# Nine bursts of plain fp32 products instead of thirteen in two pairs of heads

## The chip, the cores and the metric

The kernel runs on one core of one Trainium2 chip. The metric is the device time of one execution in microseconds (us); lower is better. The core has a tensor engine (TensorE, PE in the profile), a vector engine (VectorE, DVE), a scalar engine (ScalarE, ACT), GpSimd (POOL) and SyncE (SP), which issues the transfers. Each engine runs its own queue of instructions in order and meets the others by semaphores.

## The reference

One layer of a streaming encoder over 4096 tokens of width 1024, all in float32:

```python
h = rms_norm(x, norm_g)
proj = einsum('bsd,de->bse', h, w_in)         # 5376 columns
(qa, ka, va, za, qb, kb, vb, zb, ga, gb) = split(proj, ...)
ya = swa_sink_attention(rope(qa), rope(ka), va, a_sinks) * silu(za)   # 8 q heads, 2 kv heads, own chunk + 1 back
yb = chunked_relpos_attention(qb, kb, vb, b_rel_bias) * silu(zb)      # 8 heads, own chunk + 8 back
merged = sigmoid(ga + gate_bias0) * (ya @ w_br_a) + sigmoid(gb + gate_bias1) * (yb @ w_br_b)
out = rms_norm(x + merged @ w_out, final_g)
```

A chunk is 64 tokens and a head 64 wide. Branch A sees a window of two chunks and has a sink term in its softmax; branch B sees nine chunks and adds a bias by relative position.

## The kernel before

The sequence is worked in eight blocks of 512 tokens (`NBLK`), each block four query tiles of 128 (`TT`). The first and last block are written out, the six between run in a loop (`blocks`, L639). The projections are made with two-part numbers: each factor is split into a high part and a rest in the type fp32r, and three products (hi hi, lo hi, hi lo; L909 to L911, L876 to L878 and L851 to L853) stand for one fp32 product. In what follows R is one such product of 512 columns. A weight tile is worked in four quarters of six R each; a quarter is the step `("mm", tile, quarter)`.

The attention is made in plain fp32. Heads are taken two at a time: four A pairs (sets 0 to 3) and four B pairs (sets 4 to 7), in the order 0, 4, 1, 5, 2, 6, 3, 7 (`ORDER`). For a pair TensorE makes
- S, `scores` (L944 for A, L953 for B): the score tile of one query tile, into the PSUM tiles `sc`; the VectorE shapes it (mask, bias) and takes the row maxima (L1242 to L1268), the ScalarE makes the exponentials (`exps`, L1146), which are E in the plan and free the score tile;
- T, `turn_p` (L973): up to four 128x128 transposes of the probabilities into `ps_pt`. ScalarE (L1153) or VectorE (L1329), as `A_OUT` and `B_OUT` say, copies them into a ring of four tiles `probs_t`. A turn waits until the turn before it is copied out;
- V, `values` (L1004): products of the turned probabilities with the values, summed in `ps_o`. A V step takes the key blocks of one entry of `A_BURSTS` or `B_BURSTS`. V3 of an A pair takes two. The first V of a pair waits until the pair before has been read out of `ps_o` (`whole`, L1366);
- N, `norm` (L1013): four transposes of the reciprocal sums into an accumulator bank, from which VectorE makes `gate` (L1360).

The order of all this is written out by hand. `block_plan` (L130) makes one list of steps, `PLAN`, and every engine walks the same list and issues its own part of each step. `A_BEATS` (L119) and `B_BEATS` (L120) are the beats of one pair: T, V, S and E as above with their numbers, F the next quarter of a weight tile from the list `fill`, G and H the gating of the pair before, D the denominators. S and E in a pair's beats belong to the next pair. `norm` is put in by a rule: after the fourth F or later, when the quarter left its tile open. Twelve F belong to a pair. Jobs that hang on a tile travel with its quarters: after the last quarter of a q tile of branch A ScalarE makes `pre` and `pre_hi` (L1098, L1101); the next tile's first quarter carries `rope_in` (VectorE: L1304, L1308) and its third the rope products (TensorE: L1024, L1025). A rope product takes the bank that `norm` used last, and waits till `gate` has read it. For the second A pair (set 1) these are the rope of q2, in tile z5.

`check_ring` (L345) holds the plan to the rule that a turn's ring slot has been read by its V step four turns later.

Of the kernel before, what the change touches and what calls it, by code (L numbers as in the profile page):

```python
# [24 lines left out]
D = 1024  # L25
# [90 lines left out]
O_BANKED = 2  # L116


A_BEATS = "T0 F G T1 V0 F H D T2 V1 S0 F E0 T3 V2 F S1 V3 F E1 F F S2 F E2 F F S3 F E3 F"  # L119
B_BEATS = "F T0 F G T1 F H D T2 V0 F T3 F T4 V1 S0 F T5 E0 F T6 V2 S1 F T7 E1 F T8 V3 S2 F T9 E2 V4 S3 T10 F E3 V5 F V6"  # L120
BEATS_QUARTERS = 12
NORM_AFTER = 4
EARLY = 1
# [6 lines left out]
def block_plan():  # L130
# [45 lines left out]
    for n, s in enumerate(ORDER):  # L176
        nxt = ORDER[n + 1] if n + 1 < SETS else None
        quarters = 0
        for beat in (A_BEATS if s < PAIRS else B_BEATS).split():
            kind, no = beat[0], int(beat[1:] or 0)  # L180
# [1299 lines left out]
```

## Time and profile before

| | before |
|---|---|
| median of three executions | 3417.24 us (3415.64 to 3418.3) |
| profiled execution, its own time | 3415.78 us |
| its span from first to last instruction | 3414.0 us |
| TensorE matmuls busy | 3342.3 us, 98% |
| VectorE, ScalarE, GpSimd busy | 1488.9, 1422.8, 1306.6 us |
| mean granted TensorE clock | 0.999 |

Busy TensorE time is made of modelled ends and contains overlaps of neighbouring matmuls; the time from one start to the next is what a matmul takes of the span. A row of the timeline has the start and the duration in us, the engine, the line of the kernel, the operation, output and inputs, the shapes, how many instructions of the same kind were merged into the row, and in brackets the idle time before it with what ended it.

### The profile page before, as it was taken

What the parts mean: (1) busy time and instruction counts of PE and PEld (TensorE: products, weight loads), DVE (VectorE), ACT (ScalarE), POOL (GpSimd) and SP (SyncE); (2) the same over time, 40 slices, a digit from 0 to 9 for tenths busy, and PEclk for the clock granted to TensorE, in tenths of its full rate; (3) what the DMA queues carried; (4) which work ended last, traced back from release to release, by engine and by line L of the source; (5) the groups of instructions that cost most, each with busy time, mean ns of one, the idle gap of its engine ahead of it and who ended that gap; (6) DMA issues with size and microseconds to landing.
All of it is one profiled execution on the core that took longest, in us unless ns stands there. A gap on an engine that the chain in (4) does not pass through costs nothing.

```text
span 3414.0 us, 48305 instructions
## 1 busy us (share of the span) xinstructions
PE 3342.3 (98%) x16328; PEld 2498.0 (73%) x16328; DVE 1488.9 (44%) x3097; ACT 1422.8 (42%) x2969; POOL 1306.6 (38%) x1087
## 2 busy tenths in 40 slices
PE   8999999999999999999999999999999999999998
PEld 6667876678766787667876678766787667876676
DVE  4662355513555135551355513555135551355512
ACT  4443444434444344443444434444344443444432
POOL 3334442345423454234542344423454234542244
PEclk9999999999999999999999999999999999999999
DMA  4222431224311242112421124311242112521123
GB/s 156 62 62 87 172 99 50 62 87 167 99 50 62 87 168 99 50 62 87 168 99 52 61 86 168 98 56 61 83 172 94 55 60 84 173 93 56 56 82 116
DMA packets 97782, 319.53 MB, mean 94 GB/s; under 512 B 9984, under 2 KB 26624, under 8 KB 95360
## 3 DMA queue, kind: packets, MB, share of 16 engines
q1 hardware_dynamic: 97536, 316.34, 28.4%
q8 instruction: 144, 2.36, 0.3%
q14 instruction: 102, 0.84, 0.1%
HBM read 299.52 MB, written 16.78 MB: 93 GB/s over the span
## 4 chain that ended last, share of the span: by engine, by line
PE 85%; issue 6%; DVE 5%; POOL 2%; ACT 1%; DMA 0%; DVEq 0%; POOLq 0%; SPq 0%; ACTq 0%
PE acc L909 16%; PE acc L911 14%; PE acc L910 14%; PE ps_o L1004 6%; PE ps_pt L973 5%; PE sc L953 4%; PE sc L909 3%; PE sc L910 3%; PE sc L911 3%; POOL w_lo L755 2%; PE sc L944 2%; PE sc L851 2%; PE sc L852 2%; PE sc L853 2%; PE sc L876 1%
## 5 line engine op out<-in xcount | busy, mean ns | idle before, releaser
L755 POOL TENSOR_TENSOR w_lo<-w_raw,w_hi 128x512 fp32r<-128x512 f32 x928 | 1209.2, 1309 | 2060.0 <-ACT w_hi L1058 2059.3
L909 PE MATMUL acc<-h_hi,w_hi 128*128 128x512 f32 x2432 | 1010.4, 415 | 2.4 <-DVE q L1316 2.4
L911 PE MATMUL acc<-h_hi,w_lo 128*128 128x512 f32 x2432 | 952.7, 392 | 0.0
L910 PE MATMUL acc<-h_lo,w_hi 128*128 128x512 f32 x2432 | 950.4, 391 | 0.0
L1058 ACT ACTIVATE w_hi<-w_raw 128x512 fp32r<-128x512 f32 x928 | 574.2, 624 | 392.9 <-DMA w_raw<-w 116.5
L909 PEld LDWEIGHTS acc<-h_hi,w_hi 128*128 128x128 f32 x2432 | 456.3, 188 | 212.3 <-issue 133.9
L911 PEld LDWEIGHTS acc<-h_hi,w_lo 128*128 128x128 f32 x2432 | 456.4, 188 | 101.5
L910 PEld LDWEIGHTS acc<-h_lo,w_hi 128*128 128x128 f32 x2432 | 458.1, 188 | 75.7
L1146 ACT ACTIVATE probs_b<-sc,negm 128x640 f32<-128x640 f32 x256 | 203.2, 794 | 373.6 <-DVE negm L1263 373.0
L1153 ACT ACTIVATE probs_t<-ps_pt 128x512 f32<-128x512 f32 (+1 forms) x272 | 150.7, 554 | 264.8 <-PE ps_pt L973 264.8
L1288 DVE SCALAR_TENSOR_TENSOR part<-th,sc 128x512 f32<-128x512 f32 x64 | 43.9, 686 | 468.0 <-PE sc L911 467.8
L1329 DVE COPY probs_t<-ps_pt 128x512 f32<-128x512 f32 (+1 forms) x188 | 125.3, 666 | 250.8 <-PE ps_pt L973 250.3
L1263 DVE TENSOR_REDUCE negm<-sc 128x1 f32<-128x640 f32 x256 | 211.0, 824 | 8.9
L909 PE MATMUL sc<-y_hi,w_hi 128*128 128x512 f32 x512 | 201.5, 394 | 6.0 <-DVE y_lo L1376 6.0
L911 PE MATMUL sc<-y_hi,w_lo 128*128 128x512 f32 x512 | 199.4, 389 | 0.0
L910 PE MATMUL sc<-y_lo,w_hi 128*128 128x512 f32 x512 | 199.3, 389 | 0.0
L973 PE MATMUL ps_pt<-ident,probs_b 128*128 128x128 f32 x1200 | 187.0, 274 | 6.2 <-DVE probs_t L1329 6.2
L973 PEld LDWEIGHTS ps_pt<-ident,probs_b 128*128 128x128 f32 x1200 | 147.6, 141 | 52.9 <-DVE probs_t L1329 8.6
L1255 DVE TENSOR_TENSOR sc<-sc,bias 128x256 f32<-128x256 f32 (+2 forms) x512 | 184.3, 360 | 3.0
L1116 ACT ACTIVATE th<-acc,gb_half 128x512 f32<-128x512 f32 x128 | 88.1, 688 | 218.4 <-PE acc L911 218.4
L1004 PE MATMUL ps_o<-probs_t,v_b 128*64 128x512 f32 (+1 forms) x960 | 175.9, 455 | 1.0 <-DVE probs_t L1329 0.3
L953 PE MATMUL sc<-k_b,q 64*128 64x320 f32 (+3 forms) x992 | 164.3, 448 | 3.6 <-ACT probs_b L1146 3.6
(140 smaller groups left out, 3923.8 us busy)
## 6 DMA issues: line engine op xcount, KB each, us to landing
w_raw<-w SPq DMA_DIRECT2D x464, 512.0 KB, 3.5
rows<-x SPq DMA_DIRECT2D x36, 512.0 KB, 7.4
xt<-x_t SPq DMA_DIRECT2D x16, 1024.0 KB, 10.0
out<-rows SPq DMA_DIRECT2D x32, 512.0 KB, 2.8
x_in<-x SPq DMA_DIRECT2D x28, 512.0 KB, 5.4
cs<-rope_tab SPq DMA_DIRECT2D x8, 512.0 KB, 4.3
bias<-near SPq DMA_DIRECT2D x1, 1024.0 KB, 13.3
g_out<-final_g SPq DMA_DIRECT2D x1, 512.0 KB, 11.5
```

Source lines behind the costliest of these rows:

```text
L755: pool.tensor_tensor(w_lo[n % 2][:, c], w_raw[n % 2][:, c], w_hi[n % 2][:, c].bitcast(FP32), ALU.subtract).then_inc(w_split, 1)
L909: pe.matmul(dst[:, :], hi, src_hi[:, k, :], start=begin, stop=False)
L910: pe.matmul(dst[:, :], hi, src_lo[:, k, :], start=False, stop=False)
L911: mm = pe.matmul(dst[:, :], lo, src_hi[:, k, :], start=False, stop=end)
L953: mm = pe.matmul(sc[hh][:, c, lo:B_HALF], q[n % 2][rows_, t * P:(t + 1) * P], k_b[rows_, s - PAIRS, t * P + c * B_HALF + lo:t * P + (c + 1 ...
L973: mm = pe.transpose(ps_pt[:, col + (t - t0) * P:col + (t - t0 + 1) * P], weights_of(s, hh, t)[:, r * P:(r + 1) * P], ident[:, :])
L1004: mm = pe.matmul(ps_o[HD * hh:HD * hh + HD, t0 * P:(t0 + n) * P], val, ring(first, turn)[:, col:col + n * P], start=j == every[0], stop=j ...
L1058: act.activation(w_hi[n % 2][:, c], w_raw[n % 2][:, c], ACT.Copy).then_inc(w_hi_done, 1)
L1146: act.activation(p_, score_tile(s, hh, t), ACT.Exp, bias=negm[:, POS[s] % 2, c:c + 1], accum_out=sums[:, POS[s] % 2, c:c + 1]).then_inc(pr ...
L1153: act.activation(ring(first, turn)[:, 0:n], ps_pt[:, 0:n], ACT.Copy).then_inc(pt_out[0], 1)
L1255: dve.tensor_tensor(dst, dst, tab, ALU.add).then_inc(scores_shaped, 1)
L1263: dve.tensor_reduce(nm, score_tile(s, hh, t), AX.XY, ALU.max, negate=True).then_inc(neg_ready, 1)
```

## The change

Two strings of beats are replaced. No function and no other constant is changed.

```diff
-A_BEATS = "T0 F G T1 V0 F H D T2 V1 S0 F E0 T3 V2 F S1 V3 F E1 F F S2 F E2 F F S3 F E3 F"
-B_BEATS = "F T0 F G T1 F H D T2 V0 F T3 F T4 V1 S0 F T5 E0 F T6 V2 S1 F T7 E1 F T8 V3 S2 F T9 E2 V4 S3 T10 F E3 V5 F V6"
+A_BEATS = "T0 F G T1 F H D T2 V0 V1 S0 F E0 T3 F F S1 V2 V3 F E1 F S2 F E2 F F S3 F E3 F"
+B_BEATS = "F T0 F G T1 F H D T2 F T3 F V0 V1 S0 T4 F T5 E0 F T6 V2 S1 F T7 E1 F T8 V3 S2 F T9 E2 V4 S3 T10 F E3 F V5 V6"
```

In an A pair V0 moves behind T2, directly ahead of V1; V2 moves behind S1, directly ahead of V3; and one F moves from between E1 and S2 to ahead of S1. In a B pair V0 moves from behind T2 to ahead of V1, T4 moves from ahead of V1 to behind S0, and V5 moves behind the last F, directly ahead of V6. Counted as stretches with V or S between two F, an A pair has four instead of six and a B pair five instead of seven.

## Rows read from the trace of the kernel before

**Rows 1.** Page of the profile: busy time by engine, and granted clock in 40 slices.
```profile
PE 3342.3 (98%) x16328; PEld 2498.0 (73%) x16328; DVE 1488.9 (44%) x3097; ACT 1422.8 (42%) x2969; POOL 1306.6 (38%) x1087
...
PEclk9999999999999999999999999999999999999999
```
**Rows 2.** TensorE's timeline (start, us, line, operands, count): four turns between products R.
```profile
562.54 0.39 PE L910 MATMUL acc<-h_lo,w_hi 128*128 128x512 f32 x1
562.77 0.40 PE L911 MATMUL acc<-h_hi,w_lo 128*128 128x512 f32 x1
563.00 0.60 PE L973 MATMUL ps_pt<-ident,probs_b 128*128 128x128 f32 x4
563.35 0.48 PE L909 MATMUL acc<-h_hi,w_hi 128*128 128x512 f32 x1
563.67 0.39 PE L910 MATMUL acc<-h_lo,w_hi 128*128 128x512 f32 x1
```
**Rows 3.** TensorE's timeline: a lone V step of one key block between products R.
```profile
588.69 0.40 PE L911 MATMUL acc<-h_hi,w_lo 128*128 128x512 f32 x1
589.02 0.65 PE L1004 MATMUL ps_o<-probs_t,v_b 128*64 128x256 f32 x4
589.60 0.50 PE L909 MATMUL acc<-h_hi,w_hi 128*128 128x512 f32 x1
589.94 0.40 PE L910 MATMUL acc<-h_lo,w_hi 128*128 128x512 f32 x1
```
**Rows 4.** TensorE's timeline: turns, then a V step, then S0 of the next pair.
```profile
536.83 0.60 PE L973 MATMUL ps_pt<-ident,probs_a 128*128 128x128 f32 x4
537.36 0.65 PE L1004 MATMUL ps_o<-probs_t,v_a 128*64 128x256 f32 x4
537.94 1.35 PE L953 MATMUL sc<-k_b,q 64*128 64x320 f32 x8
```
**Rows 5.** TensorE's timeline: a V step of two key blocks, then turns.
```profile
590.88 0.39 PE L911 MATMUL acc<-h_hi,w_lo 128*128 128x512 f32 x1
591.20 0.66 PE L1004 MATMUL ps_o<-probs_t,v_b 128*64 128x128 f32 x8
591.79 0.66 PE L973 MATMUL ps_pt<-ident,probs_a 128*128 128x128 f32 x4
...
592.52 0.39 PE L910 MATMUL acc<-h_lo,w_hi 128*128 128x512 f32 x1
```
**Rows 6.** TensorE's timeline: V0 of the third A pair; T4 of the third B pair.
```profile
595.02 0.65 PE L1004 MATMUL ps_o<-probs_t,v_a 128*64 128x256 f32 x4 [0.75 <-DVE whole L1366]
...
630.13 0.40 PE L911 MATMUL acc<-h_hi,w_lo 128*128 128x512 f32 x1
630.70 0.55 PE L973 MATMUL ps_pt<-ident,probs_b 128*128 128x128 f32 x3 [0.18 <-DVE probs_t L1329]
```
**Rows 7.** Timelines of TensorE, ScalarE and VectorE in the second A pair, S0 being in Rows 4.
```profile
543.41 1.35 PE L953 MATMUL sc<-k_b,q 64*128 64x320 f32 x8
549.91 0.49 PE L1024 MATMUL acc<-pre_hi,perm_r 128*128 128x512 f32 x1 [1.17 <-DVE gate L1360]
...
544.75 0.63 ACT L1101 ACTIVATE pre_hi<-pre 128x512 fp32r<-128x512 f32 x1
548.50 0.19 ACT L1146 ACTIVATION_READ_ACCUMULATOR probs_b<-sc,negm 128x1 f32 x1
...
544.86 0.11 DVE L1252 MEMSET sc<- 64x64 f32 x1 [2.55 <-PE sc L953]
547.70 0.68 DVE L1304 TENSOR_TENSOR pre_lo<-pre,pre_hi 128x512 fp32r<-128x512 f32 x1
549.09 0.68 DVE L1360 TENSOR_TENSOR gate<-acc,z 128x512 f32<-128x512 f32 x1
```
**Rows 8.** TensorE's timeline: S1 and S2 in the first A pair of a block.
```profile
484.41 1.35 PE L953 MATMUL sc<-k_b,q 64*128 64x320 f32 x8
491.04 1.35 PE L953 MATMUL sc<-k_b,q 64*128 64x320 f32 x8
```

## The prediction

> **What bounds the kernel.** The page comes first: TensorE is busy 98% of the span, VectorE 44%, ScalarE 42%, GpSimd 38%, and the granted clock is in its highest tenth in all forty slices, so the 2.4 GHz level [rows 1]. A step on another engine is therefore worth only the wait that it gives TensorE; a step on TensorE is worth its own time. The change moves no instruction out of the kernel, so the question is what TensorE loses between instructions. For that I read its timeline by starts, not by durations (the durations overlap: products start every 0.23 us and are shown as 0.39). Then I read ScalarE's and VectorE's timelines at the places where the order changes.
>
> **What a burst costs.** In a run of split products (R, 512 columns) starts are 0.23 us apart. A burst of four turns T between two R takes 562.77 to 563.67, 0.90 us from the R before to the second R after, of which 2 x 0.23 is what two R cost anyway: 0.44 for four turns, 0.11 each [rows 2]. A lone `values` step V takes 588.69 to 589.94, 1.25 us, less 0.46 for two R: 0.79. Its own columns are 4 x 256, at 2.4 GHz 0.43 us. So 0.36 us is spent in getting in and out: 0.10 before V (0.33 from R to V against 0.23), 0.16 behind its columns (0.59 to the next start against 0.43), 0.10 in the first R behind it (0.34 against 0.23) [rows 3]. Next to a turn V saves nothing: 0.53 from T to V is the turns' 0.44 and again 0.09, and V to the score tile S is 0.58 [rows 4]. But inside one V step there is no such gap: V6 of a B pair is two key blocks, eight pieces of 128 columns (V3 of an A pair has the same form), the same 0.43 us of columns, and the next group starts 0.59 us after it, as it does after a V of one block. A burst in which T follows the V takes 590.88 to 592.52, 1.64 us, less 0.46, 0.44 and 0.43: 0.31, so T behind V gives back 0.05 [rows 5].
>
> **The plan, part by part.** I wrote out both plans step by step. The instructions are the same; what changes is the neighbours.
> - A pairs: V0 goes from behind T1 to in front of V1, and V2 from behind T3 to in front of V3 (one F, a quarter tile of six R, moves ahead of S1). Two V steps lose their borders.
> - B pairs: V0 and V1 become neighbours behind F, with T4 now behind them; V5 moves next to V6. In the last B pair of a block V5 and V6 are neighbours already.
> - So a block has 4 x 2 + 3 x 2 + 1 = 15 joins V-V. Block 0 leaves out V steps without keys: 8 + 3 = 11. In all 7 x 15 + 11 = 116 joins.
>
> The trace has no V-V border with a wait between the steps. Its cost lies between 0 (the border inside V6, whose loads and products are of the same shape) and 0.16 (V to another kind) [rows 5]. I take 0, the nearest row, so each join saves 0.36 [rows 3]: 116 x 0.36 = 41.8 us. T4 stands behind products in 4 B pairs of 7 blocks: 28 x 0.05 = 1.4 us.
>
> A page rule speaks against this. The Trainium skill, TensorE: Matmul & The Clock Gate, section Part 3 (Packing small matmuls), says that a weight load overlaps running matmuls only when its row group differs; neighbouring V steps use all rows, so by it their loads would not hide. By that page the border V-V would stay unhidden and the rival with 0.16 per join would be right; the eight pieces of [rows 5], whose stationary operands change within the step with no time lost, speak against it.
>
> **Waits that go.** V0 of the third A pair waits for VectorE's `whole` with 0.75 us idle, one of eight such rows [rows 6]. In the new plan V0 stands a quarter tile and four turns later (1.8 us), so 8 x 0.75 = 6.0 us go. T2, which is next, needs T1's copy: VectorE makes it directly behind `whole`, and V5's 0.43 us ahead of T0 put T1 later relative to the chain that starts at the q tile's end, so nothing is late there. In the third B pair T4 starts 0.57 us after the last R instead of 0.23, because T3's copy on VectorE is late; seven such rows [rows 6]. Now V0 (0.8 us and more) lies between: 7 x 0.34 = 2.4 us go. T4 to T5 is now turns, one F and `norm`, no less than T0 to T1, where the same ScalarE copy is in time.
>
> **A wait that grows.** A step list per engine shows one change of order on VectorE: in the second A pair the F that carries `rope_in` for q2 moves ahead of S1, so its two VectorE operations (L1304, L1308) are now queued ahead of the shaping of S1. Behind them wait S1's maxima, its exponentials, `norm`'s product (`gate`, L1360), and for that the rope product on TensorE (L1024), which needs its bank. S0 to S1 is 5.47 us and S0 to the rope product 11.97 [rows 4, 7]. ScalarE finishes `pre_hi` at 544.75 + 0.63 = 545.38 (it is behind S0's exponentials, which do not move). L1304 then starts at 545.42; the two operations hold VectorE 1.39 us (547.70 to 549.09), so the shaping starts at 546.81 instead of 544.86, takes its 2.84 us (544.86 to 547.70), `gate` starts at 549.65 and the rope product 0.82 us behind that, at 550.47. That is 12.53 us after S0, 0.56 later than before, where the sum above booked a gain of 0.36 for the join V2-V3. Correction 0.92 x 8 blocks = 7.4 us. TensorE itself would be there 10.3 us after S0 (5.47 - 0.79 + 1.37 to S1, then the 5.69 of the next part less one F), so it is this chain that counts.
>
> ScalarE has one change: a split of the next weight tile stands ahead of tile 1's exponentials in each A pair. It fits into the idle time before these (they wait for VectorE), so it costs nothing; uncovered it would cost some 0.6 us, as long as `pre_hi` of the same shape takes [rows 7]. GpSimd's and SyncE's orders are unchanged.
>
> **The distance that gets short.** In A pairs S2 waits for the exponentials of tile 1, and S1 to S2 shrinks: 6.63 us now, less six R (1.37), plus V2 (0.43): 5.69 [rows 8]. S1 to the end of those exponentials is 543.41 to 548.69, 5.28 us [rows 7]. 0.41 us are left, so I book nothing. In the second pair the rope wait hides it. This is the thinnest cover, 32 times in the kernel.
>
> **Sum.** 41.8 + 1.4 + 6.0 + 2.4 - 7.4 = 44.2 us. The profiled execution's span is 3414.0 us and its own time 3415.8, 1.5 below the median of 3417.2. From the span 3369.8, from the median 3373.0 us.
>
> **Rivals.**
> 1. V-V keeps a border of 0.16 us. For it: every border of V to something else has it, and the second V has a wait in front. Against: the border inside V6. 116 x 0.16 = 18.6 us less gain: 3391.6 us.
> 2. S2 comes late in A pairs. If the chain from S1 grows by 0.75 us (one more 0.7 us operation on VectorE), 32 x (0.75 - 0.41) = 11 us: 3384 us. For it: 0.41 us is less than one VectorE operation. Against: the per-engine order shows none added but in the second pair.
> 3. The rope chain costs nothing, because `rope_in` turns out earlier than I read: 3365.6 us. Against: ScalarE is behind S0's exponentials.
> 4. The change does not do what it says: the 0.36 us belongs to each V step, wherever it stands. Then only the waits move, 6.0 + 2.4 - 7.4: 3416 us. Against: the 0.10 in front and the 0.10 behind lie outside the V.
> 5. Slower: the chain S1, maxima, exponentials, S2 becomes the bound of every A pair. It decides from 44.2 / 32 + 0.41 = 1.8 us of added chain; with the two operations of the second pair (1.39) and one more product like L1360 (0.68) ahead of S1 everywhere it would be 2.07: 32 x 1.66 = 53 us lost against 44.2 gained, 3426 us. Against: only one pair of four carries a `rope_in` there.
>
> **Chances.** Forecast 0.67; rival 1 0.14; rival 2 0.09; rival 3 0.05; rival 4 0.03; rival 5 0.02. The range reaches from rival 3 to rival 1 with some 2 us of error on either side: 3363 to 3394 us. A measurement of this kernel can tell about 0.2% (7 us) from no change; faster by more than that is the forecast and rivals 1 to 3, 0.95; within it rival 4, 0.03; slower rival 5, 0.02.
>
> **What would show it.** In the profile after, V1 of an A pair should start 0.43 us behind V0; 0.59 there is rival 1. The third A pair's 0.75 wait and T4's wait should be gone. The wait of the rope product for `gate` should grow from 1.17 to some 2.3 us. S2 of A pairs should show no wait for `probs_b`; one of 0.3 is rival 2. The clock should stay in its highest tenth. I would be wrong if a copy out of `ps_pt` or the ring of four came late at a place where I read only the order.

## The result and the profile after

| | before | after |
|---|---|---|
| median of five executions | 3416.75 us | 3398.23 us (3396.62 to 3398.9) |
| ratio to before | | 0.9945, 95% interval 0.9932 to 0.9958 |
| span of the profiled execution | 3414.0 us | 3396.7 us |
| mean granted TensorE clock | 0.999 | 0.994 |

The change makes the kernel 18.5 us faster. The forecast was 44.2 us faster, and the time lies outside its range of 3363 to 3394 us. The page after, first the busy time by engine, then the granted clock in 40 slices:

```profile
PE 3314.0 (98%) x16328; PEld 2511.9 (74%) x16328; DVE 1491.5 (44%) x3097; ACT 1423.9 (42%) x2969; POOL 1310.7 (39%) x1087
...
PEclk9999999999999999999999999999999999999999
```

Against [rows 1] nothing stands out. 85 us slices do not show what lasts 3 us, and TensorE is still called 98% busy. The mean clock of 0.994 beside 0.999 is the first hint: half a percent of the span is 17 us, which is some 34 us more at half the clock.

**The joins came as forecast.** TensorE's timeline after, second A pair (T2 V0 V1 S0, then S1 V2 V3), and second to last the join V0 V1 of the first B pair:

```profile
536.80 0.60 PE L973 MATMUL ps_pt<-ident,probs_a 128*128 128x128 f32 x4
537.33 1.08 PE L1004 MATMUL ps_o<-probs_t,v_a 128*64 128x256 f32 x8
...
544.42 1.35 PE L953 MATMUL sc<-k_b,q 64*128 64x320 f32 x8
545.70 1.09 PE L1004 MATMUL ps_o<-probs_t,v_a 128*64 128x256 f32 x12
546.72 0.50 PE L909 MATMUL acc<-h_hi,w_hi 128*128 128x512 f32 x1
...
512.41 1.94 PE L1004 MATMUL ps_o<-probs_t,v_b 128*64 128x512 f32 x8
514.28 0.59 PE L944 MATMUL sc<-k_a,q 64*128 64x192 f32 x4
```

V2 and V3 are one row of twelve instructions and take 545.70 to 546.72, 1.02 us. Their columns are 2 x 0.43, and what is left is the one exit of 0.16 known from [rows 3]. The B join takes 1.87 us to the next start for 8 x 512 columns (1.71) and again 0.16. So the border V-V costs nothing, with a satisfied wait between the steps.

**The rope product of the second A pair lost it.** VectorE's, GpSimd's and TensorE's timelines after, the place of [rows 7]:

```profile
545.82 0.72 DVE L1304 TENSOR_TENSOR pre_lo<-pre,pre_hi 128x512 fp32r<-128x512 f32 x1 [3.10 <-ACT pre_hi L1101]
546.64 1.59 DVE L1308 TENSOR_TENSOR pre<-pre,cs 128x512 f32<-128x512 f32 x1
548.31 0.11 DVE L1252 MEMSET sc<- 64x64 f32 x1
551.14 0.68 DVE L1360 TENSOR_TENSOR gate<-acc,z 128x512 f32<-128x512 f32 x1
...
546.38 1.30 POOL L755 TENSOR_TENSOR w_lo<-w_raw,w_hi 128x512 fp32r<-128x512 f32 x1 [0.40 <-ACT w_hi L1058]
...
551.95 0.66 PE L1024 MATMUL acc<-pre_hi,perm_r 128*128 128x512 f32 x1 [3.14 <-DVE gate L1360]
```

S0 starts at 538.35 here, so the rope product stands 13.60 us behind it; the forecast said 12.53, and before it was 11.97. L1304 starts 7.47 us after S0, where 7.48 was forecast. L1308 takes 1.59 us instead of the 0.69 that goes with its shape: GpSimd's w_lo began at 546.38 and ends at 547.68, and L1308 ends 0.55 us later. From there everything is one chain: shaping, `gate`, rope product. TensorE is idle for 3.14 us, not the 2.3 forecast and not the 1.17 of before.

**And then the clock fell.** The same place one block later, after:

```profile
975.35 0.79 PE L1024 MATMUL acc<-pre_hi,perm_r 128*128 128x512 f32 x1 [3.14 <-DVE gate L1360]
976.36 0.63 PE L909 MATMUL acc<-h_hi,w_hi 128*128 128x512 f32 x1
976.79 0.63 PE L910 MATMUL acc<-h_lo,w_hi 128*128 128x512 f32 x1
...
978.95 1.35 PE L953 MATMUL sc<-k_b,q 64*128 64x320 f32 x8
```

Two R start 0.43 us apart where 0.23 is usual. The rope product to S2 takes 3.60 us; with the clock up it is 2.01 (before: 549.91 to 551.92). The views of chosen windows, the 3 us from the rope product on, for two blocks of the kernel after and then one of the kernel before. The third number from the right is the granted clock:

```profile
975.40:978.40 3.00, 3.00 (x7) 2.44 (x8) 1.38 (x2) 0.66 (x3) 1.28 (x1) 0.50 0.02 5
2246.60:2249.60 3.00, 3.00 (x16) 2.09 (x16) 1.83 (x2) 0.69 (x3) 1.29 (x1) 1.00 0.02 5
```

```profile
549.90:552.90 3.00, 2.99 (x16) 2.11 (x16) 1.66 (x2) 0.00 (x0) 1.92 (x2) 1.00 0.41 106
```

A clock of 0.50 is 1.2 GHz. It fell behind this wait in six of the eight blocks after and in none before; in two blocks the same idle time of 3.1 us left it up. What a fall costs is read from the rope product to that of the third pair, TensorE's timeline after, first a block with a fall and then one without:

```profile
1822.54 0.79 PE L1024 MATMUL acc<-pre_hi,perm_r 128*128 128x512 f32 x1 [3.14 <-DVE gate L1360]
1873.12 0.50 PE L1024 MATMUL acc<-pre_hi,perm_r 128*128 128x512 f32 x1
...
2246.58 0.49 PE L1024 MATMUL acc<-pre_hi,perm_r 128*128 128x512 f32 x1 [3.15 <-DVE gate L1360]
2294.32 0.50 PE L1024 MATMUL acc<-pre_hi,perm_r 128*128 128x512 f32 x1
```

That is 50.58 us against 47.74. Two blocks (1822.54 and 2669.08) lose 2.85 us in this way, and their clock stands at half for some 6.7 us; the other four falls last some 3.4 us and cost 1.5 to 1.6 us each. The six together are 11.9 us.

### The profile page after: what moved, and what is told of

It is laid out like the page before. It is cut to its first block, busy times and chain, and to the rows that moved or that the text cites. A ratio compares the mean times of both kernels' runs of the same rounds, so it can differ in the third digit from the quotient of the medians.

```text
span 3396.7 us, 48305 instructions
## 1 busy us (share of the span) xinstructions
PE 3314.0 (98%) x16328; PEld 2511.9 (74%) x16328; DVE 1491.5 (44%) x3097; ACT 1423.9 (42%) x2969; POOL 1310.7 (39%) x1087
## 4 chain that ended last, share of the span: by engine, by line
PE 82%; issue 9%; POOL 4%; DVE 3%; ACT 2%; DMA 0%; POOLq 0%; DVEq 0%; SPq 0%; ACTq 0%
PE acc L909 15%; PE acc L911 14%; PE acc L910 14%; PE ps_o L1004 5%; PE ps_pt L973 5%; POOL w_lo L755 4%; PE sc L953 4%; PE sc L909 3%; PE sc L911 3%; PE sc L910 3%; PE sc L944 2%; PE sc L853 1%; PE sc L852 1%; PE sc L851 1%; PE sc L876 1%
## 5 line engine op out<-in xcount | busy, mean ns | idle before, releaser
L1146 ACT ACTIVATE probs_a<-sc,negm 128x256 f32<-128x256 f32 x256 | 120.1, 474 | 109.5 <-DVE negm L1268 108.8
```

The lines of the kernel that those rows point to most:

```text
L1146: act.activation(p_, score_tile(s, hh, t), ACT.Exp, bias=negm[:, POS[s] % 2, c:c + 1], accum_out=sums[:, POS[s] % 2, c:c + 1]).then_inc(pr ...
```

## The experiments

The theory was: the joins and the vanished waits are worth what was forecast (51.6 us), and the loss is in one place per block, in two parts, the longer wait of the rope product and the clock behind it. The rival: the joins are worth about half, everywhere, which would give 18 us just as well.

**One string at a time.** `B_BEATS` alone:

```diff
+B_BEATS = "F T0 F G T1 F H D T2 F T3 F V0 V1 S0 T4 F T5 E0 F T6 V2 S1 F T7 E1 F T8 V3 S2 F T9 E2 V4 S3 T10 F E3 F V5 V6"
```

> Only B_BEATS is changed, A_BEATS is that of before. Theory (each join V-V saves 0.36 us; the loss sits at the rope product of the second A pair, which this kernel leaves alone): 52 joins x 0.36 + 28 x 0.05 + seven T4 waits x 0.34 = 22.5 us faster than before, 3392 to 3397 us, so faster than the changed kernel although it makes half of the change; the rope product's wait stays at 1.17 us and the granted clock at 0.999. Rival (each join saves only half as much, everywhere): some 12 us faster than before, 3402 to 3407 us.

Measured: 3391.41 us, 24.8 us faster than before (ratio 0.9927, 0.9909 to 0.9944), and 7 us faster than the whole change; that is 0.6 us below the band of 3392 to 3397. The rope product waits as before and the clock is 0.999:

```profile
547.82 0.49 PE L1024 MATMUL acc<-pre_hi,perm_r 128*128 128x512 f32 x1 [1.17 <-DVE gate L1360]
```

`A_BEATS` alone:

```diff
+A_BEATS = "T0 F G T1 F H D T2 V0 V1 S0 F E0 T3 F F S1 V2 V3 F E1 F S2 F E2 F F S3 F E3 F"
```

> Only A_BEATS is changed, B_BEATS is that of before. Theory (64 joins x 0.36 + 8 V0 waits x 0.75 = 29 us gained, 8 x 3.6 = 29 us lost at the rope product of the second A pair: 1.6 by its wait, 1.6 by the clock behind it, 0.36 of a join's gain that is covered): no change to 4 us slower, 3413 to 3421 us; wait of the rope product about 3.1 us, clock about 0.52 in the 2 us behind it. Rival (each join saves half): 9 us faster, 3405 to 3410 us.

Measured: 3423.01 us, 6.8 us slower than before (ratio 1.0019, 1.0009 to 1.0029), 2 us beyond the band. The clock fell behind the rope product in all eight blocks, not six:

```profile
553.98 0.79 PE L1024 MATMUL acc<-pre_hi,perm_r 128*128 128x512 f32 x1 [3.15 <-DVE gate L1360]
```

Half of the change holds more than the whole gain, the other half is a loss; together they give 24.8 - 6.8 = 18.0 us, the 18.5 of the whole. The rival falls by the B half: half-priced joins would have given it some 12 us, and no rope wait hides anything there.

**GpSimd taken out of the way.** The changed kernel with ScalarE's order of before:

```diff
-... S1 V2 V3 F E1 F S2 ...
+... S1 V2 V3 E1 F F S2 ...
```

> The changed kernel with E1 ahead of the F in A_BEATS (S1 V2 V3 E1 F F S2): nothing moves on TensorE or VectorE; on ScalarE the split of the next weight tile goes back behind tile 1's exponentials, and so GpSimd's w_lo goes away from VectorE's rope operations. Theory (L1308 took 1.59 us instead of 0.69 because it ran into a w_lo on GpSimd): L1308 0.7 us, rope product 12.5 us after S0 instead of 13.6, wait 2.1 us. If the clock then holds its upper level 8 x 2.6 = 21 us faster than the changed kernel, 3375 to 3380 us; if it still falls 8 x 1.0: 3388 to 3392 us. Rival (L1308 is slow for another reason): 3398 us and a wait of 3.1 us.

Measured: 3384.98 us, 13 us less than the change. VectorE's, GpSimd's and TensorE's timelines:

```profile
545.88 0.69 DVE L1308 TENSOR_TENSOR pre<-pre,cs 128x512 f32<-128x512 f32 x1
...
543.96 1.27 POOL L755 TENSOR_TENSOR w_lo<-w_raw,w_hi 128x512 fp32r<-128x512 f32 x1 [6.90 <-ACT w_hi L1058]
551.09 1.30 POOL L755 TENSOR_TENSOR w_lo<-w_raw,w_hi 128x512 fp32r<-128x512 f32 x1 [5.86 <-ACT w_hi L1058]
...
550.30 0.49 PE L1024 MATMUL acc<-pre_hi,perm_r 128*128 128x512 f32 x1 [2.24 <-DVE gate L1360]
```

No w_lo lies beside L1308 and it takes 0.69 us again; the wait is 0.9 us shorter. So the 0.9 us were the collision, set off by the one split that the forecast priced at nothing. The time lies between the two bands given, because the clock neither held everywhere nor fell everywhere: behind the rope product it fell in four of eight blocks (the first, whose wait is 3.77 us, and three of the seven with 2.2 us). Two of these windows:

```profile
550.30:553.30 3.00, 3.00 (x16) 2.10 (x16) 1.84 (x2) 1.23 (x4) 2.21 (x2) 1.00 0.02 5
971.10:974.10 3.00, 2.97 (x10) 1.96 (x11) 1.82 (x2) 1.26 (x4) 2.18 (x2) 0.69 0.02 5
```

**VectorE's order of before.** The changed kernel with `rope_in` of set 2 one quarter later:

```diff
-            fill[at_] = [*fill[at_], ("rope_in", s)]
+            late = at_ + (s == 2)
+            fill[late] = [*fill[late], ("rope_in", s)]
```

> The changed kernel with rope_in of the second A pair one quarter later, so behind S1's shaping in VectorE's order, as in the kernel before; ScalarE's order stays changed. Theory: shaping starts 1.45 us after S1, rope product 6.5 us after S1 (as before: 543.41 to 549.91), so about 12.55 us after S0 instead of 13.6, wait 2.1 to 2.2 us, clock held: 3375 to 3381 us. Rival (the order on VectorE alone costs nothing, only its collision with GpSimd, which may come back at another operation): 3385 us or more.

Measured: 3381.42 us (ratio 0.99, 0.9883 to 0.9918), half a microsecond above the band. The rope product:

```profile
547.17 0.50 PE L1025 MATMUL acc<-pre_hi,perm_r 128*128 128x512 f32 x1 [2.10 <-DVE gate L1361]
```

The wait is 2.10 us, as expected of this run, and the clock fell in three of eight blocks. So with either repair the step that the forecast had worked out (12.53 us after S0, 2.3 us of wait) is there (12.56 us here, 12.71 with GpSimd out of the way); but even that wait is long enough for the clock to fall now and then, a cost that it did not have.

**The wait itself taken away.** The changed kernel with that `rope_in` behind S1 and the rope product one weight tile later, where `norm`'s product has long been read:

```diff
-            fill[at_] = [*fill[at_], ("rope_in", s)]
+            late = at_ + (s == 2)
+            fill[late] = [*fill[late], ("rope_in", s)]
+            at_ += 4 * (s == 2)
             fill[at_ + 2] = [("rope", s), *fill[at_ + 2]]
```

> The changed kernel with rope_in of the second A pair behind S1 (as in rope_in_late) and the rope product one weight tile later, behind S3, where norm's product has long been read; the first A pair has the same pattern. Theory (the loss is all in the wait of the rope product and the clock that falls behind it): no wait of 2 us at the rope product, clock 0.999, in its place 0.3 to 0.5 us at the next tile's claim as in the first pair; 8 x 2.2 - 8 x 0.4 + the clock of three of eight blocks (3 x 1.6) = 19 us below rope_in_late, 3358 to 3367 us. Rival (another wait takes its place, at S2 or S3 of that pair): 3372 us or more.

Measured: 3360.74 us, inside the band of 3358 to 3367, 55.8 us faster than before (ratio 0.9836, 0.9822 to 0.9849) and 37 us faster than the change. The rope product follows its score tile with no wait, and a short one stands at the next tile's claim:

```profile
549.77 1.35 PE L955 MATMUL sc<-k_b,q 64*128 64x320 f32 x8
551.05 0.50 PE L1026 MATMUL acc<-pre_hi,perm_r 128*128 128x512 f32 x1
...
554.86 0.49 PE L911 MATMUL acc<-h_hi,w_hi 128*128 128x512 f32 x1 [0.35 <-DVE q L1318]
```

The same move of the rope product in the kernel before, to price it apart:

```diff
+            at_ += 4 * (s == 2)
             fill[at_ + 2] = [("rope", s), *fill[at_ + 2]]
```

> The kernel before with its rope product of the second A pair one weight tile later, nothing else. It takes the wait of 1.17 us (1.4 us against an unhindered start) and may bring 0.3 to 0.5 us at the next claim: 8 x 1.0 = 8 us faster than before, 3406 to 3412 us. It prices what the change and the move of the rope product do apart from each other: if theory holds, the joins and the two other waits (51.6 us) stand on top of it.

Measured: 3409.24 us, inside the band and 7.4 us faster than before (ratio 0.9978, 0.9969 to 0.9988). The two kernels without the rope wait differ by 3409.24 - 3360.74 = 48.5 us, and the forecast's sum without its rope term is 41.8 + 1.4 + 6.0 + 2.4 = 51.6. That is the change's own worth outside the rope product, and it is right within 3 us.

**Which resource the wait hung on.** The rope product moved, but `rope_in` left ahead of S1 and the split ahead of E1:

```diff
+            at_ += 4 * (s == 2)
             fill[at_ + 2] = [("rope", s), *fill[at_ + 2]]
```

> The changed kernel with the rope product one weight tile later, but rope_in still ahead of S1 on VectorE and the split still ahead of E1 on ScalarE. The bank no longer waits, but S1's shaping is still late by 1.4 us for the two operations and 0.9 us for GpSimd. Theory: the chain S1, maxima, exponentials, S2 is then 7.5 us against 5.7 us of TensorE's work, so S2 of that pair waits some 1.8 to 2.0 us for probs_b (the forecast's rival 2 in one pair of four) and the clock falls behind it in about two to four of eight blocks: 3376 to 3386 us. Rival (only the bank mattered): no wait at S2, same as rope_later, 3358 to 3367 us.

Measured: 3388.69 us, some 3 us above the band. The bank no longer matters and S2 waits in its place:

```profile
551.17 1.35 PE L954 MATMUL sc<-k_b,q 64*128 64x320 f32 x8 [2.00 <-ACT probs_b L1147]
```

Behind these 2.0 us the clock fell in four of seven blocks, and in the first, where the wait is 3.59 us. The late shaping of S1 is one cause with two receivers: take the bank away and the exponentials are next. It is the forecast's rival 2, in the one pair of four that the per-engine order had pointed to.

## Why the prediction was wrong, step by step

- *A lone V has 0.36 us around it and a join saves all of it*: right. The border V-V is 0, as the pieces within one V had shown; rival 1 and the page's rule that loads hide only where row groups differ (the Trainium skill, TensorE: Matmul & The Clock Gate, Part 3) do not hold for these steps. The B half gave 24.8 us where 18.7 + 1.4 + 2.4 = 22.5 stood; the 2.3 us more are not traced.
- *The waits of V0 and T4 go*: right, no row of either is left after.
- *S2 keeps 0.41 us in A pairs*: right in the running blocks. In the first block, where VectorE has more to fill in, S2 of the first pair waits 0.95 us against 0.24 to 0.28 in the kernels with the A pairs of before.
- *The rope product 12.53 us after S0*: its place and mechanism were right, its size was not. It measured 13.60, 1.07 us more in each block, 8.6 us in all.
- *ScalarE's split ahead of E1 costs nothing*: **this step failed**. I asked whether ScalarE had idle time for it, and it had. I did not follow what the split sets off: GpSimd's w_lo, 1.30 us, now beside a VectorE operation on the critical chain. With the split back in its place L1308 takes 0.69 us instead of 1.59 and the wait 2.24 us instead of 3.14: 0.9 of the 1.07 us in each block. The kernel before shows the same collision, in the rows under this list. I read durations of each engine in its own lane and did not ask why one of them was twice the usual.
- *The clock stays up*: **this step failed** too. The wait of 1.17 us had never cost clock, and I took the grown wait at its own length. The six falls behind it cost 11.9 us. Even with the wait as forecast, at 2.1 to 2.25 us, the clock fell in three of eight and in four of eight blocks.
- What I overlooked: in the third A pair tile k7 moves ahead of S1 as well, and claims the bank that the rope product used before VectorE has read it. In the first block that is the row below (TensorE's timeline after), 1.1 us; later blocks lose 0.13 us each (T3 to S1 is 3.44 us there and 3.30 in the second pair). 2 us in all.

```profile
194.38 0.50 PE L909 MATMUL acc<-h_hi,w_hi 128*128 128x512 f32 x1 [1.11 <-DVE q L1316]
```

The collision as the kernel before has it, VectorE's and GpSimd's timelines: `y_lo`, of the same shape as L1308, takes 1.40 us beside w_lo.

```profile
535.47 1.40 DVE L1376 TENSOR_TENSOR y_lo<-whole,y_hi 128x512 fp32r<-128x512 f32 x1
...
535.04 1.29 POOL L755 TENSOR_TENSOR w_lo<-w_raw,w_hi 128x512 fp32r<-128x512 f32 x1 [2.85 <-ACT w_hi L1058]
```

One more fall stands far from the change. The start of the second weight tile of the execution, TensorE's timeline and the view of a chosen window, first before and then after:

```profile
25.53 0.50 PE L876 MATMUL sc<-w_hi,h_hi 128*128 128x512 f32 x1 [0.92 <-POOL w_lo L755]
26.40:29.40 3.00, 3.00 (x15) 2.45 (x14) 3.00 (x4) 0.00 (x0) 2.88 (x3) 1.00 0.46 143
...
25.57 0.50 PE L876 MATMUL sc<-w_hi,h_hi 128*128 128x512 f32 x1 [2.07 <-POOL w_lo L755]
26.40:29.40 3.00, 3.00 (x9) 2.33 (x8) 3.00 (x4) 0.00 (x0) 2.89 (x3) 0.51 0.53 152
```

The tile starts at the same time in both, as it waits for w_lo; the idle time is longer after because TensorE's last product ahead of it started at 23.12 us instead of 24.23. The wait itself costs nothing. But behind it the clock fell, and the first rope product of the block stands 1.65 us later than before (51.84 against 50.19). This is not the change's doing: the kernel before with only its rope product moved waits 2.25 us there, and its clock fell too.

The sum anew: 44.2 - 8.6 (rope product later) - 1.1 (in the first block its wait grew by 3.1 us, from 1.59 to 4.66, where later blocks have 2.0) - 11.9 (six falls) - 2 (tile k7) - 1.6 (the fall at the start) = 19.0 us. Measured are 18.5 us by the medians and 17.3 by the spans of the two profiled executions. The falls are counted in one execution; the mean clock of the other four is 0.994 as well. Why the clock fell in some blocks and not in others with the same wait stays open.

## What to carry to other kernels

When steps are moved against each other in a shared plan, write out the order of every engine before and after, and follow each changed entry one engine further, to what it releases; a split that is free on its own engine can start a neighbour that blocks a third. On a kernel whose TensorE is 98% busy, price a growing TensorE wait above its own length: here the shortest wait with a fall of the clock behind it was 2.00 us, and each fall cost 1.5 to 2.9 us more. And join products of the same shape: borders between kinds cost 0.1 to 0.2 us each, borders within a kind nothing.

## What the runs showed of the hardware

- The granted clock of TensorE and the idle time ahead, counted over six kernels at the rope product and in a seventh, where that was moved, at S2: with 1.09 to 1.59 us idle it fell in none of 16 cases (before, B half alone); with 2.0 to 2.25 us in ten of 21 (three of seven, three of seven, four of seven); with 3.1 us in twelve of fourteen; at 3.59 us and over in four of four. The one case with 2.52 us kept it. At the start of the second weight tile it fell in none of four kernels with 0.92 to 1.45 us idle and in all five with 2.03 to 2.37. When it fell it stood at half for some 3.4 us in most cases, and for some 6.7 us in two blocks of the kernel after.
- In the first microseconds of an execution the view's clock column can't be relied on: it gives 1.00 while products R start 0.43 us apart (after: 16.74 and 17.17), the distance that they have elsewhere at 0.50.
- A VectorE operation with two inputs in SBUF (L1308) stood still while GpSimd ran its w_lo: it took 1.59 us where w_lo had begun 0.26 us earlier, and ended 0.55 us after it. Without the neighbour it took 0.69. The Trainium skill, SBUF — State Buffer, section "SBUF: two separate sides", says that the two engines take a shared port pair as an exclusive lock, and that the one that comes second waits for the whole instruction; the trace agrees, with 0.9 us lost.
